# Weights of the attention mixer read from contiguous 8 KB pieces, and its products spread to one per slot

## The reference

```python
# layer 0: retention + short convolution (first mixer), then the expert FFN, on all six tiles
# layer 1: windowed attention (second mixer), then the expert FFN, on the four latent tiles
q, k, v = split(a_lat @ w_in)          # 1024 -> 1024 | 256 | 256; context tiles need k and v alone
q, k = rope(q), rope(k)
probs = softmax([q k^T over 384 window keys, q k_ctx^T over 256 context keys, sink])   # 16 heads, 4 kv heads
out = (probs @ v) @ w_out               # 1024 -> 1024
h = h + gate * out

# expert FFN (PEER), for each token: 8 heads x top 16 of 128 x 128 product keys
act = gelu(sum(xn * u_tab[expert], -1))
y = sum_k (gate_k * act_k) * v_tab[expert_k]     # 128 experts for each token
```

## Time and profile before

| what | value |
|---|---|
| median of 3 runs | 4095.4 us (4089.33 to 4099.39) |
| the profiled execution | 4092.54 us, span 4090.8 us |
| TensorE matmuls, VectorE, GpSimd, ACT busy | 71%, 63%, 39%, 33% of the span |
| all DMA | 1478.38 MB, mean 361 GB/s |
| the gathers' queue | 184704 packets, 1342.31 MB, 81.8% of 16 engines |
| SyncE's queue | 46800 packets, 133.31 MB, 9.5% |
| DMAs of w_in, w_out of the second mixer | 144 and 128, 128 KB each |

### The profile page before, as it was taken

One profiled execution on the slowest core, in us unless ns is written; L12 is line 12 of the kernel. 1 busy time (PEld: TensorE's weight loads), 2 busy tenths in 40 slices (PEclk: granted clock), 3 DMA queues, 4 the chain that ended last, 5 costly groups with the idle time before them and its releaser, 6 DMA issues. The chain is left out here.

```text
span 4090.8 us, 41461 instructions
## 1 busy us (share of the span) xinstructions
PE 2896.1 (71%) x14677; PEld 981.6 (24%) x14677; DVE 2569.6 (63%) x5990; ACT 1365.2 (33%) x3356; POOL 1592.5 (39%) x1411
## 2 busy tenths in 40 slices
PE   4999856667668667666877687677868766766665
PEld 0794611111112111111232133122412311111110
DVE  3313378875874885785486566746765677587444
ACT  2220123333333323233253354333625423333222
POOL 0005024444444543443343344434435444444332
PEclk7998877778768668767878798788878877866666
DMA  9117279999999999999999999999899999999998
GB/s 363 52 62 279 101 291 421 421 414 421 416 408 393 420 413 385 421 420 390 348 369 335 395 388 349 368 375 376 330 334 400 371 373 421 421 420 410 421 421 340
DMA packets 231824, 1478.38 MB, mean 361 GB/s; under 512 B 30112, under 2 KB 30160, under 8 KB 60992
## 3 DMA queue, kind: packets, MB, share of 16 engines
q0 software_dynamic: 184704, 1342.31, 81.8%
q1 hardware_dynamic: 46800, 133.31, 9.5%
q10 hardware_dynamic: 112, 0.11, 0.0%
HBM read 1470.29 MB, written 5.34 MB: 361 GB/s over the span
## 5 line engine op out<-in xcount | busy, mean ns | idle before, releaser
L1422 PE MATMUL peer_py<-peer_ring,peer_diag 64*64 64x512 f32 x10240 | 1834.5, 815 | 981.2 <-ACT peer_diag L1231 908.0
L1179 POOL DMA_INDIRECT peer_ring<-in_uv_dram,peer_idx x1280 | 1461.5, 1142 | 2037.2 <-PE peer_py L1422 1893.1
L1691 DVE CUSTOM_DVE_ANT_0 peer_ring<-peer_ring,peer_f 128x1024 f32<-128x1024 f32 x1280 | 1554.1, 1226 | 824.0 <-DMA peer_ring<-in_uv_dram,peer_idx 809.0
L1227 ACT ACTIVATE peer_diag<-peer_stack,peer_u 128x64 f32<-128x64 f32 x1280 | 443.6, 347 | 2057.7 <-DVE peer_u L1691 2037.1
L1422 PEld LDWEIGHTS peer_py<-peer_ring,peer_diag 64*64 64x64 f32 x10240 | 350.7, 163 | 2311.8 <-ACT peer_diag L1231 1999.4
L1231 ACT ACTIVATE peer_diag<-peer_diag,peer_gate 128x64 f32<-128x64 f32 x1280 | 445.1, 348 | 46.6
L1392 PE MATMUL peer_pb<-arena,peer_fT 128*128 128x512 f32 x320 | 186.4, 674 | 1.2 <-ACT peer_fT L1199 1.2
L355 DVE TENSOR_TENSOR m_w_low<-m_w_low_plain,m_w_high 128x2048 fp32r<-128x2048 f32 x16 | 37.4, 2338 | 170.5 <-ACT m_w_high L350 170.5
L1553 PE MATMUL mix_ps<-mod_rows_sb,peer_mix_aT 128*128 128x512 f32 x128 | 87.5, 800 | 67.5 <-DMA mod_rows_sb<-in_od_w_out_dram 67.5
L1778 DVE CUSTOM_DVE_ANT_0 peer_mix_flat<-mix_ps,peer_mix_mask,peer_mix_sink 128x512 f32<-128x512 f32 (+1 forms) x64 | 52.2, 816 | 107.8 <-PE mix_ps L1506 97.6
L1691 DVE DVE_READ_ACCUMULATOR2_ANT peer_u<- 128x1 f32 x1280 | 105.1, 82 | 0.0
(11 more groups left out here) (208 smaller groups left out, 2745.0 us busy)
## 6 DMA issues: line engine op xcount, KB each, us to landing
mod_rows_sb<-in_ada_w_dram SPq DMA_DIRECT2D x33, 1024.0 KB, 5.0
peer_ring<-in_uv_dram,peer_idx POOLq DMA_INDIRECT x1280
mod_rows_sb<-in_od_w_in_dram SPq DMA_DIRECT2D x144, 128.0 KB
mod_rows_sb<-in_od_w_out_dram SPq DMA_DIRECT2D x128, 128.0 KB
arena<-in_ada_w_dram SPq DMA_DIRECT2D x15, 1024.0 KB, 16.2
m_w_low_plain<-in_ev_w_in_dram SPq DMA_DIRECT2D x12, 1024.0 KB, 5.2
arena<-in_peer_wq_dram SPq DMA_DIRECT2D x2, 4096.0 KB, 29.1
mod_rows_sb<-mod_rows SPq DMA_DIRECT2D x10, 512.0 KB, 6.7
```

The source lines that it names most:

```text
L1179: pool.indirect_dma_start(ring[:, n % RING], None, A["uv"], bass.IndirectOffsetOnAxis(idx[:, i % 2, hd, k:k + 1], 0)).then_inc(sem(f"lande ...
L1227: act.activation(diag[:, n % RING], stack[:], ACT.Gelu, scale=u[:, n % RING:n % RING + 1]).then_inc(sem("gelu"), 1)
L1422: ins = pe.matmul(PY[strip(c), r], diag[strip(r), n % RING], ring[strip(r), n % RING, D + c * HALF:D + (c + 1) * HALF], start=s == 0, stop ...
L1691: dve.tensor_tensor_reduce(x, x, f[:, i % 2], 1.0, 0.0, ALU.mult, ALU.add, u[:, n % RING:n % RING + 1]).then_inc(sem("dot"), 1)
```

## The change

Three things. GpSimd copies w_in and w_out during the first mixer into DRAM tensors `mix_in` and `mix_out`, in which the four rows that a partition needs for four pieces lie side by side (8 KB); each copy is waited for before the next. SyncE then loads groups of four pieces (1 MB, all 128 partitions, one DMA) into a ring of two, after one wait for all copies; TensorE waits once a group and releases it with its fourth piece. Products with one tile and outputs issue one matmul a slot; the start slots of some norms, products and attentions move by 1 to 10 slots, and VectorE reads an output half 5 slots behind its last matmul, not 2. The buffers that this needs come from others: the normalised input, its transpose and the rotated tokens lie in `flat`, the head outputs in `qT`, and the scratch of the rotation in the routing's `hot`.

```diff
+def lay_pieces(queue, S, A, mix_in, mix_out):
+    laid = 0
+    def copied(to, src):
+        nonlocal laid
+        queue.dma_start(to, src).then_inc(S("mix_laid"), 16)
+        laid += 16
+        queue.wait_ge(S("mix_laid"), laid)
+    for c in range(3):
+        for g in range(PER):
+            copied(mix_in[c, g], A["od_w_in"][0].rearrange("(g k p) n -> g p k n", g=PER, p=P)[g, :, :, c * HALF:(c + 1) * HALF])
+    for c in range(2):
+        for g in range(PER):
+            q, j = divmod(g * WG, 4)
+            for x in range(2):
+                src = A["od_w_out"][0].rearrange("(q x j n) w -> q x n j w", q=2, x=2, j=4)
+                copied(mix_out[c, g, x * HD:(x + 1) * HD], src[q, x, :, j:j + WG, c * HALF:(c + 1) * HALF])
...
         def _(pool):
             norm_shift(pool, S, T, a, rows)
+            lay_pieces(pool, S, A, mix_in, mix_out)
...
-PRODUCTS = (..., (KV, ((3, 1, 0),), at(4, 15)), (Q0, ..., at(4, 21)), (Q1, ..., at(4, 32)), ...
+PRODUCTS = (..., (KV, ((3, 1, 0),), at(4, 14)), (Q0, ..., at(4, 22)), (Q1, ..., at(4, 33)), ...
-ATTENDS = (at(4, 50), at(5, 30), at(6, 50), at(7, 8))
+WG = 4
+PER = KC // WG
+ATTENDS = (at(4, 52), at(5, 33), at(6, 52), at(7, 8))
-W_RING = 4
+W_RING = 2
 def product_slot(job, n):
-    return job[2] + 2 * n // 3
+    return job[2] + (n if len(job[1]) == 1 else 2 * n // 3)
 def out_slot(b, n):
-    return ATTENDS[b] + STEP * PAIRS + 14 + 2 * n // 3
+    return ATTENDS[b] + STEP * PAIRS + 14 + n
...
             def in_pieces(c):
-                for k in range(KC):
+                for g in range(PER):
                     to, loaded = next_slot()
-                    for x in range(2):
-                        at_row = k * P + x * HD
-                        sp.dma_start(to[x * HD:(x + 1) * HD], A["od_w_in"][0][at_row:at_row + HD, c * HALF:(c + 1) * HALF]
-                                     ).then_inc(loaded, 16)
+                    sp.dma_start(to, mix_in[c, g]).then_inc(loaded, 16)
...
             modulation_rows()
+            sp.wait_ge(S("mix_laid"), 16 * (3 + 4) * PER)
             in_pieces(KV)
...
-            def piece(first):
+            def piece(k, first):
                 n = pieces
-                if first:
-                    pe.wait_ge(S(f"mix_w{n % W_RING}"), 32 * (n // W_RING + 1))
-                return w[:, n % W_RING]
+                if first and k % WG == 0:
+                    pe.wait_ge(S(f"mix_w{n % W_RING}"), 16 * (n // W_RING + 1))
+                return w[n % W_RING][:, k % WG]
...
-                    yield out_slot(b, PAIRS * (c + 1) - 1) + 2
-                    dve.wait_ge(S("mix_w_used"), OUT_PIECES[b] + (c + 1) * PAIRS)
+                    yield out_slot(b, PAIRS * (c + 1) - 1) + 5
+                    dve.wait_ge(S("mix_w_used"), OUT_PIECES[b] + (c + 1) * PER)
```

More of the change, by code:

```diff
@@ L431, with mixer0_stage @@
 SC = P + SEQ
-def mixer0_stage(nc, S, A, h, ident, silu, mod_d, strips_d, arena, rows):
+def lay_pieces(queue, S, A, mix_in, mix_out):
[14 more added lines that the diff above has]
+                copied(mix_out[c, g, x * HD:(x + 1) * HD], src[q, x, :, j:j + WG, c * HALF:(c + 1) * HALF])
+def mixer0_stage(nc, S, A, h, ident, silu, mod_d, strips_d, arena, rows, mix_in, mix_out):
     n_in = 6
@@ L935 @@
 BAND = P + 2 * 128
-NORMS = ((0, 0, at(2, 5)), (1, 1, at(2, 15)), (2, 0, at(3, 5)), (3, 1, at(4, 4)), (4, 0, at(5, 5)), (4, 0, at(5, 100)), (5, 1, at(6, 4)))
+NORMS = ((0, 0, at(2, 5)), (1, 1, at(2, 15)), (2, 0, at(3, 5)), (3, 1, at(4, 4)), (4, 0, at(5, 5)), (4, 0, at(5, 110)), (5, 1, at(6, 4)))
 KV, Q0, Q1 = 2, 0, 1
[L940 to L944, removed]
-ATTENDS = (at(4, 50), at(5, 30), at(6, 50), at(7, 8))
+PRODUCTS = ((KV, ((0, 0, 0), (1, 1, 1)), at(2, 27)), (KV, ((2, 0, 0),), at(3, 17)), (KV, ((3, 1, 0),), at(4, 14)),
+            (Q0, ((2, 0, 1), (3, 1, 3)), at(4, 22)), (Q1, ((2, 0, 0), (3, 1, 2)), at(4, 33)), (KV, ((4, 0, 0),), at(5, 17)),
+            (KV, ((5, 1, 0),), at(6, 14)), (Q0, ((4, 0, 1), (5, 1, 3)), at(6, 22)), (Q1, ((4, 0, 0), (5, 1, 2)), at(6, 33)))
+WG = 4
+PER = KC // WG
+PRODUCT_PIECES = tuple(PER * n for n in (1, 2, 3, 4, 5, 8, 11, 12, 13))
+OUT_PIECES = tuple(PER * n for n in (5, 8, 13, 15))
+ATTENDS = (at(4, 52), at(5, 33), at(6, 52), at(7, 8))
 PAIRS = ATT_HEADS // 2
 STEP = 5
-W_RING = 4
+W_RING = 2
 def product_slot(job, n):
-    return job[2] + 2 * n // 3
+    return job[2] + (n if len(job[1]) == 1 else 2 * n // 3)
 def product_end(job):
@@ L980, in key_tiles, with trunk_stage @@
     return list(range(CT)) + [CT + j for j in range(lo, hi)]
-def trunk_stage(nc, S, A, h, ident, mod_d, arena, rows):
+def trunk_stage(nc, S, A, h, ident, mod_d, arena, rows, mix_in, mix_out):
     with ExitStack() as ctx:
@@ L995, in trunk_stage @@
         shift_row, scale_row, gate_row, mix_gate = rows[:, 0, 0], rows[:, 0, 1], rows[:, 0, 2], rows[:, 1, 0]
-        w = rows[:, 1, 1:3].rearrange("p a n -> p (a n)").rearrange("p (r n) -> p r n", r=W_RING)
+        w_own = sb("mix_w", [P, WG, HALF])
+        w = (rows[:, 1, 1:3].rearrange("p a (k n) -> p (a k) n", n=HALF), w_own[:])
         f = sb("f", [P, 2, D])
@@ L1035, in trunk_stage @@
         ms = sb("mix_ss", [P, 4, len(NORMS)])
-        aT = (aT_own, flat[:, 0:D].rearrange("p (k n) -> p k n", k=KC))
-        t1, t2, tmp = (flat[:, D + x * HALF:D + (x + 1) * HALF] for x in range(3))
+        aT = [flat[:, x * D:(x + 1) * D].rearrange("p (k n) -> p k n", k=KC) for x in range(2)]
+        norm = flat[:, 2 * D:3 * D]
+        tok = norm.rearrange("p (a n) -> p a n", a=2)
+        tmp = hot[:].rearrange("p a b c -> p (a b c)")
         pr = flat[:, 0:PR * KEYS].rearrange("p (r n) -> p r n", r=PR)
         pT = flat[:, PR * KEYS:(PR + 1) * KEYS]
-        oT = aT_own
-        norm = tok[:].rearrange("p a n -> p (a n)")
         qT = [h[:, x].rearrange("p (m n) -> p m n", m=PAIRS) for x in range(2)]
@@ L1073, in next_slot @@
                     sp.wait_ge(S("mix_w_used"), n - W_RING + 1)
-                return w[:, n % W_RING], S(f"mix_w{n % W_RING}")
+                return w[n % W_RING], S(f"mix_w{n % W_RING}")
             def in_pieces(c):
-                for k in range(KC):
+                for g in range(PER):
                     to, loaded = next_slot()
-                    for x in range(2):
-                        at_row = k * P + x * HD
-                        sp.dma_start(to[x * HD:(x + 1) * HD], A["od_w_in"][0][at_row:at_row + HD, c * HALF:(c + 1) * HALF]
-                                     ).then_inc(loaded, 16)
+                    sp.dma_start(to, mix_in[c, g]).then_inc(loaded, 16)
             def out_pieces():
                 for c in range(2):
-                    for m in range(PAIRS):
+                    for g in range(PER):
                         to, loaded = next_slot()
[L1088 to L1091, removed]
+                        sp.dma_start(to, mix_out[c, g]).then_inc(loaded, 16)
             def row(out, layer, half, kd, sec, done):
@@ L1289, in output @@
                 act.wait_ge(S("mix_o"), 2 * p + 2)
-                act.activation(oT[:, m], PM[:, 3, P:2 * P], ACT.Copy).then_inc(S("mix_oT"), 1)
+                act.activation(qT[b % 2][:, m], PM[:, 3, P:2 * P], ACT.Copy).then_inc(S("mix_oT"), 1)
             def attended(b):
@@ L1460, in product_of @@
                             pe.wait_ge(S("mix_kT"), tile + 2)
-                    weights = piece(x == 0)
+                    weights = piece(k, x == 0)
                     ins = pe.matmul(PM[:, bank], aT[to][:, k], weights, start=k == 0, stop=k == KC - 1)
-                    if x == len(parts) - 1:
+                    if x == len(parts) - 1 and k % WG == WG - 1:
                         pieces += 1
@@ L1551, in outputs @@
                         pe.wait_ge(S("mix_oT"), PAIRS * (b + 1))
[L1552 to L1555, removed]
+                    weights = piece(m, True)
+                    ins = pe.matmul(PM[:, c], qT[b % 2][:, m], weights, start=m == 0, stop=m == PAIRS - 1)
+                    if m % WG == WG - 1:
+                        pieces += 1
+                        ins.then_inc(S("mix_w_used"), 1)
             def mixer():
@@ L1714, in normed, with rope @@
                 dve.reciprocal(ms[:, 3, j:j + 1], ms[:, 2, j:j + 1]).then_inc(S("mix_rstd"), 1)
[L1716 removed]
+            def rope(cosines, ps, t, heads):
                 wide = heads * HD
+                tokens, t2 = cosines, tmp[:, 0:wide]
                 def by_head(x):
[L1722 to L1724 removed]
+                    return x.rearrange("p (x j n) -> p x j n", x=2, n=HD)
+                dve.tensor_tensor(tokens, by_head(ps), cos[:, t].rearrange("p (o q n) -> p o q n", o=1, q=1).broadcast_to([P, 2, heads // 2, HD]),
                                   ALU.mult)
@@ L1733, in rope @@
                 link(ins)
+                return dve.tensor_tensor(tokens, tokens, by_head(t2), ALU.add)
             def keys_roped(j, x):
@@ L1746, in keys_roped @@
                         dve.wait_ge(S("mix_tabs"), 64)
```

(12 more changed lines are left out.)

4 lines of the change are left out of this document (1 added, 3 removed).

## The result

The changed kernel takes 3969.5 us (median of four runs, 3964.5 to 3976.1) against 4092.4 before: ratio 0.970, 95% interval 0.968 to 0.972. Its profiled execution took 3966.0 us, span 3964.2, 126.6 less than the span of before. The forecast was 3990, in a range of 3945 to 4055.

The account below looks back on a forecast made before the run. The prediction took expert-loop slots to be bound by their bytes, with TensorE as second floor. Gains of 113 us less 6, 2 and 2 gave 103 off 4092.5, say 3990, range 3945 to 4055.

Parts of the forecast that it names:

- The reading of the bound: Expert loop: a slot costs its bytes at 421 GB/s; of 883 us in nine weight stretches, 143 are not bytes.
- rival 1: Weight stretches: the rate stays at 330 to 360 GB/s, only waits go, 33 us, 4060; chance 0.10.
- The signs that were named: Outputs at 410 GB/s or more, TensorE idle under 15 us, gather packets 280 ns, last copy before 300 us.
- The cause of the low rate: Gathers beside weights: 2 KB, 64-partition pieces, not two active queues, lose 0.94 us each, up to 128 us.
- the rule on packets: Engines take queues' packets in turn, so shares follow packet size; alone it would leave only 33 us gain, 4060.
- Small key/value stretches: Three stretches of one key/value product: 155.4 us before, bytes alone 135.0, gain 15.
- The two long ones: Two stretches with key/value and both query products: 337.3 us, TensorE second limit at 0.88, gain 31.
- rival 2: TensorE bounds wherever there are products, so long stretches give nothing: 64 us less, 4028; chance 0.11.
- Outputs: Four output stretches: 390.4 us before, bytes 315.4, gain up to 75, taken as 67.
- Readiness: Ring of two 1 MB groups: landing takes 5.0 us against 10 available; 6 us deducted for starting and switching.
- The copies: First mixer: 14 copies on GpSimd's queue fit before or behind the convolution's wait; cost 0 to 20 us, taken 2.
- rival 3: First mixer: the copies don't fit and delay the convolution, making the kernel slower, 4143; chance 0.06.

Follow-up runs that it names:

- e1: Changed kernel, each 1 MB group loaded by four DMAs of 128 partitions with 2 KB rows: 3990.9 us, ratio 0.976.
- e2: Changed kernel, each group loaded by two DMAs of 64 neighbouring partitions with 8 KB rows: 4096.1 us, ratio 1.001.
- e6: Changed kernel, each group loaded by two DMAs with 8 KB rows, one for even and one for odd partitions: 3967.6 us, ratio 0.970.
- e7: Changed kernel, each group loaded by four DMAs of 32 neighbouring partitions with 8 KB rows: 4100.8 us, ratio 1.002.
- e5: Kernel before, each 256 KB piece one DMA over 128 partitions, w_out copied; old ring, slots and 2 KB rows: 4009.1 us, ratio 0.981.
- e10: e5 with the new slots as well, still a ring of four 256 KB pieces and 2 KB rows: 3979.3 us, ratio 0.973.
- e4: Changed kernel with the old slots, output halves read 2 slots behind: 3969.4 us, ratio 0.971.
- e8: Changed kernel with w_in read straight from its input in one DMA a group, only w_out copied: 3965.0 us, ratio 0.969.

## Why the prediction was right, and where its reason was not

**The reading of the bound** held: a slot costs its bytes, and 143 us of the nine stretches were not bytes. Some 135 of them went: 742 us are left for 309.1 MB, which take 734 at 421 GB/s. The rate beside weights did not stay low, so rival 1 falls. The signs that were named came as well: GpSimd's last copy at 193 us, gather packets of 277 ns, 4.1 us of waits before the output products. Only one output stretch stays under 410 GB/s, at 403.

**The cause of the low rate** is where the prediction failed, in the step "it is the 2 KB, 64-partition pieces", from which the part on the loads kept only the row size ("8 KB is on its side"). Rows of 2 KB over all partitions, in four times as many DMAs, cost 21 us (e1); halves with 8 KB rows cost 127 (e2). Which partitions decides: even and odd ones cost nothing (e6), 32 neighbours cost what 64 do (e7). That is shown. The reason behind it is inferred: a DMA that writes neighbouring partitions on one side of 64 reaches a part of the ways into the memory only, and holds up the gathers beside it, 260 GB/s together in place of 421. The Trainium skill has this mapping (SBUF — State Buffer, Door 1: The DMA port swizzle): partitions 0 to 63 reach the eight even ports of sixteen, 64 to 127 the odd ones, and 0 to 31 the same eight as 0 to 63. e2, e6 and e7 agree with it in all three cases; a direct count of ports is in no trace here. I weighed the rule on packets and not this one, though the diff shows `to[x * HD:(x + 1) * HD]` plainly. The price was read rightly and its reason was not: the number came out because the change removed both causes at once, and the earlier trace rows priced them together. By the same theory e2 was expected at 3970, and it takes 4096.

**The terms.** Small key/value stretches: 15 forecast, 155.4 - 135.6 = 20 measured. The two long ones: 31 forecast with TensorE as second limit at a share of 0.88, 337.3 - 288.1 = 49 measured. This term was mis-sized. TensorE's busy time fell from 138.3 and 131.5 to 125.9 and 123.8 us with the granted clock up from 0.80 and 0.87 to 0.89 and 0.91, and its share of the stretch at the end is 0.84 and 0.89 with the DMA full. So it doesn't become the bound (rival 2 falls), and part of its work before was a matter of the clock. Outputs: 67 forecast, 390.4 - 318.4 = 72 measured. Sum 141 against 113, so every term was too small.

**Readiness.** A group lands 9.0 us after its issue, not 5.0: the data take about 5 us, as the even shares show, and 4 more pass around them. It was still in time, with four slots of 2.8 to 3.1 us. e5 and e10 put prices on it: from halves to whole pieces 82 us, then 30 for the spread slots, then 10 for large groups with long rows, which is hardly more than the noise. With large groups the slots bring nothing (e4). So readiness can be had by slots or by ring. The slot edits that I priced inside the output term bring nothing in this kernel.

**The rule on packets** that the prediction cites held for the shares (0.87 to 0.84 MB with equal packets). Its worry, gathers at half pace while a group lands, cost nothing beyond the bytes.

**The copies** took 76 us where 85 to 204 were bounded, and 124 us of wait remained; rival 3 falls. Copies of 1 MB land in 5.8 us and of 0.5 MB in 4.3. The prediction's estimate from the Trainium skill (DMA: Bandwidth & Descriptors, Anatomy of one DMA), 52 us, was too low, since its 2.0 us plus bytes make 4.4 and 3.2. The copies do not show in the time. Both kernels reach the convolution together (313.74 and 313.78), long after the last copy. The first dot comes at 547.1 before the change, at 551.3 in the changed kernel and at 542.4 in e6, which has the same fourteen copies; what makes it vary between runs stays open.

The second tile starts at 869.3 in e6 and at 878.6 in e2, since the first tile takes 327 or 336 us:

```profile
542.40:869.30 326.90, 211.16 (x1116) 48.35 (x1120) 277.01 (x753) 110.24 (x281) 146.56 (x127) 0.74 1.01 420
```

```profile
542.70:878.60 335.90, 216.11 (x1116) 47.79 (x1120) 276.78 (x753) 110.36 (x281) 148.70 (x127) 0.72 1.01 409
```

These 9 us are the halves once more. The first two groups of weights are issued at 570 us, and from 580 to 600 us e6 (first) and e2 (second) run like this:

```profile
580.00:600.00 20.00, 13.83 (x70) 4.58 (x70) 13.49 (x40) 6.00 (x14) 7.64 (x7) 0.73 1.01 421
```

```profile
580.00:600.00 20.00, 9.49 (x46) 3.36 (x42) 6.39 (x18) 3.91 (x8) 4.69 (x5) 0.67 1.02 238
```

At 238 in place of 421 GB/s, 20 us lose 8.7. In e7, with quarters, the first tile takes 334.8 us and the same 20 us run at 264 GB/s.

**The deduction for unknown costs** (10 us in all) came near: 141 in the stretches became 127 in the span. But 6 of the 14 between them are the bytes that moved and 3 the varying start, so this is luck in part.

## What to carry to other kernels

When two streams of DMAs run together and the engines are full but the rate is low, look at which partitions each DMA writes before looking at row sizes: a tile loaded as two halves of 64 neighbouring partitions cost 127 us here, where short rows with more DMAs cost 21. Compare with a case that differs in one thing alone; a neighbouring row that differs in two will price the change well and explain it wrongly. And a long wait at the end of a chain (VectorE's 114.5 us) is not a price until something that removes it has been timed.

## What was not expected of the hardware

- A DMA over 64 or 32 neighbouring partitions slows another queue too: gather packets of 8 KB go from 277 to 425 ns (e2), and the total from 421 to about 260 GB/s (e2, e7); in even and odd partitions it does not (e6).
- Rows of 2 KB beside 8 KB packets cost little when all partitions are written: 415 to 417 in place of 419 to 421 GB/s in the first two stretches (e1, e8), 402 to 414 in place of 420 and 421 in the two long ones.
- A 1 MB load beside a saturated queue lands 9.0 us after its issue, of which the data are about 5, by an estimate from its share of the rate.
- TensorE's granted clock rose from 0.80 to 0.89 in a stretch where its waits for weights went, and its busy time for the same work fell by 12 us.
